# One program instead of two for the expert mixer of each layer of a decoder trunk

## The reference

```python
q = (xc @ w_q).reshape(ch, PEER_HEADS, 2, half)              # 8 heads, two halves of 128
s = jnp.einsum('thpd,hpnd->thpn', q, sub_keys)               # 128 keys a half
v1, i1 = lax.top_k(s[:, :, 0], PEER_TOPK)                    # 16 best of each half
v2, i2 = lax.top_k(s[:, :, 1], PEER_TOPK)
cand = (v1[..., :, None] + v2[..., None, :]).reshape(ch, PEER_HEADS, PEER_TOPK * PEER_TOPK)
vals, ci = lax.top_k(cand, PEER_TOPK)                        # 16 experts of 16384 for each token and head
e = (jnp.take_along_axis(i1, ci // PEER_TOPK, axis=-1) * N_KEYS + jnp.take_along_axis(i2, ci % PEER_TOPK, axis=-1))
g = jax.nn.softmax(vals, axis=-1)
act = jax.nn.gelu(jnp.einsum('td,thkd->thk', xc, u_tab[e])) * g
return jnp.einsum('thk,thkd->td', act, v_tab[e])
```

## Time and profile before

| | us |
|---|---|
| median of 3 runs (lowest, highest) | 3793.93 (3787.05, 3796.61) |
| the profiled execution | 3791.96 |
| its span, first to last instruction | 3790.2 |
| TensorE busy | 3232.8 (85%) |
| VectorE busy | 2058.1 (54%) |
| GpSimd busy | 1852.5 (49%) |
| ScalarE busy | 1267.4 (33%) |
| 768 scatters of gates, line 1700 | 1237.8, of one 1.612 |

### The profile page before, as it was taken

The page is one execution under the profiler, slowest core; times in us unless marked ns, Lnnn a source line. Parts: engine busy times, 40 slices in busy tenths (PEclk is TensorE's granted clock), DMA queues, the critical chain, the costliest instruction groups (busy, mean ns, idle before and its releaser), DMA issues. The chain is left out here.

```text
span 3790.2 us, 47486 instructions
## 1 busy us (share of the span) xinstructions
PE 3232.8 (85%) x14962; PEld 2615.9 (69%) x14962; DVE 2058.1 (54%) x4064; ACT 1267.4 (33%) x1877; POOL 1852.5 (49%) x1315
## 2 busy tenths in 40 slices
PE   8769999601999999999799889999503999999999
PEld 6558888501888888888566568888403888888887
DVE  4546677500322488888436637767400222588888
ACT  3433434200343333333325623443200222333333
POOL 0002887877870355555000004887877750455553
PEclk9889999855999999999899989999756999999999
DMA  9313656423674699999831014665423664799998
GB/s 334 123 68 115 133 123 139 86 0 30 144 182 153 228 349 351 354 351 333 293 109 45 12 38 123 147 130 124 70 0 55 144 187 146 265 349 354 349 352 295
DMA packets 396864, 680.85 MB, mean 180 GB/s; under 512 B 145008, under 2 KB 237168, under 8 KB 396528
## 3 DMA queue, kind: packets, MB, share of 16 engines
q1 hardware_dynamic: 191728, 494.73, 38.5%
q0 software_dynamic: 155648, 134.82, 18.0%
q10 hardware_dynamic: 49408, 50.33, 4.0%
HBM read 559.79 MB, written 119.93 MB: 179 GB/s over the span
## 5 line engine op out<-in xcount | busy, mean ns | idle before, releaser
L1700 POOL DMA_INDIRECT gate_matrix<-pe_misc x768 | 1237.8, 1612 | 1147.0 <-DVE pe_misc L1999 851.6
L398 PE MATMUL up_ps<-up_hhi,up_hi 128*128 128x512 f32 x2048 | 800.3, 391 | 400.2 <-PEq L1741 400.2
L389 DVE TENSOR_TENSOR up_lo<-up_raw,up_hi 128x1024 fp32r<-128x1024 f32 x256 | 313.8, 1226 | 1129.9 <-ACT up_hi L385 1047.5
L398 PE MATMUL up_ps<-up_hlo,up_hi 128*128 128x512 f32 x2048 | 798.6, 390 | 0.0
L398 PE MATMUL up_ps<-up_hhi,up_lo 128*128 128x512 f32 x2048 | 798.2, 390 | 0.0
L398 PEld LDWEIGHTS up_ps<-up_hhi,up_hi 128*128 128x128 f32 x2048 | 385.5, 188 | 480.3 <-issue 401.0
L2173 PE MATMUL ex_psy<-ex_vh,ex_ah 128*128 128x512 f32 x1536 | 600.3, 391 | 6.3 <-DVE ex_al L2274 6.1
L2173 PE MATMUL ex_psy<-ex_vl,ex_ah 128*128 128x512 f32 x1536 | 597.9, 389 | 0.0
L2173 PE MATMUL ex_psy<-ex_vh,ex_al 128*128 128x512 f32 x1536 | 597.8, 389 | 0.0
L1718 POOL DMA_INDIRECT ex_gz<-gelu,ga_at x256 | 343.5, 1342 | 387.5 <-DMA gelu<-up_z 310.0
L406 ACT ACTIVATE up_z<-up_ps 128x512 f32<-128x512 f32 x256 | 153.3, 599 | 1122.7 <-PE up_ps L398 1089.8
(11 more groups left out here) (345 smaller groups left out, 3502.6 us busy)
## 6 DMA issues: line engine op xcount, KB each, us to landing
up_raw<-in_uT SPq DMA_DIRECT2D x256, 512.0 KB
ro_wq<-in_v SPq DMA_DIRECT2D x256, 512.0 KB
gelu<-up_z SPq DMA_DIRECT2D x256, 256.0 KB
gate_matrix<-ga_at ACTq DMA_DIRECT2D x16, 3072.0 KB, 19.1
pe_misc<-gelu SPq DMA_DIRECT2D x256, 192.0 KB
ex_gm<-gate_matrix SPq DMA_DIRECT2D x128, 384.0 KB
ro_wq<-in_peer_wq SPq DMA_DIRECT2D x32, 512.0 KB
gate_matrix<-pe_misc POOLq DMA_INDIRECT x768
```

The source lines that it names most:

```text
L389: dve.tensor_tensor(self.lo[:, a, :, :], self.raw[:, a, :, :], self.hi[:, a, :, :].bitcast(F32), ALU.subtract).then_inc(self.lo_ready.sem, 1)
L398: last = pe.matmul(self.ps[:, a, :], w[:, a, dc, :], h[:, dc, :], start=(dc == 0 and m == 0), stop=(dc == DC - 1 and m == 2))
L1700: pool.indirect_dma_start(gmat.rearrange("p k (t a) -> (p k t) a", a=1), bass.IndirectOffsetOnAxis(ap=to[:, j:j + 1], axis=0), gates[:, j: ...
```

## The change

`route` and `experts` become one function, `peer`, with one block. The body of `route` stands in front of that of `experts` on each engine, in the same order. The large buffers of `route` become views of buffers of `experts` (`gv`, `vh`, `vl` and the PSUM of the v products), the small ones are allocated as before. The first head has 4 u tiles (`R0`), so its queries of the next head come after two tiles, and 68 u tiles follow the heads. In the first head VectorE makes the four `up.low`s after its first, second, fifth and last step. ScalarE's exponentials come after the third tile there. GpSimd writes all heads in one loop, waits for the gates of each, and the 48 DMAs of head 0 carry no `compute_op`.

```diff
+R0 = 4
-G0 = PH * RT
+G0 = R0 + (PH - 1) * RT
-ROUTED = 6
+def tile(h, first=False):
+    return 0 if first else h * RT + (R0 - RT)
     def scatter(self, pool, gmat, to, gates, h):
-        if h > 0:
-            pool.wait_ge(self.scattered.sem, self.scattered.base + 16 * HW * h)
+        place = gmat.rearrange("p k (t a) -> (p k t) a", a=1)
+        if h == 0:
+            for j in range(HW):
+                pool.indirect_dma_start(place, bass.IndirectOffsetOnAxis(ap=to[:, j:j + 1], axis=0), gates[:, j:j + 1], None
+                                        ).then_inc(self.scattered.sem, 16)
+            return
+        pool.wait_ge(self.scattered.sem, self.scattered.base + 16 * HW * h)
         for j in range(h * HW, (h + 1) * HW):
...
-def experts(k, l, x, up, ga, misc, wq, zmat, gmat, to, gates, rope):
+def peer(k, l, x, up, ga, misc, wq, wq_loaded, zmat, gmat, to, gates, rope):
...
+        wqh, wql = (x[:, 0, :, :].rearrange("p a (c m) -> p a c m", c=DC) for x in (vh, vl))
+        flat = gv[:].rearrange("p b d -> p (b d)")
+        sc, sc2 = (flat[:, n * D:(n + 1) * D].rearrange("p (b t n) -> p b t n", b=2, t=TT) for n in range(2))
+        cand = flat[:, 2 * D:3 * D].rearrange("p (t a b) -> p t a b", t=TT, a=TOPK)
+        cand2 = flat[:, 3 * D:4 * D].rearrange("p (t a) -> p t a", t=TT)
+        hot = flat[:, 4 * D:5 * D].rearrange("p (n a) -> p n a", a=TOPK)
+        q = flat[:, 5 * D:6 * D].rearrange("p (b t) -> p b t", b=2)
+        sk = flat[:, 6 * D:6 * D + 2 * NK].rearrange("p (b n) -> p b n", b=2)
+        psq = psy[:, 0:2, :]
+        pss = psy[:, 2:4, :].rearrange("p b (t n) -> p b t n", t=TT)
...
         def _(pe):
+            def head(h, more, first=False):
+                n = R0 if first else RT
+                scores(h)
+                for j in range(n):
+                    up.product(pe, tile(h, first) + j, j % GT)
+                    if more and j == n // 2 - 1:
+                        queries(h + 1)
+            queries(0)
+            head(0, True, first=True)
+            with pe.Fori(1, PH - 1) as h:
+                head(h, True)
+            head(PH - 1, False)
...
         def _(pool):
-            for h in range(ROUTED, PH):
+            for h in range(PH):
+                pool.wait_ge(given.sem, given.done(h))
                 ga.scatter(pool, gmat, to, gates, h)
...
         def _(dve):
+                def low(j, of_first=None):
+                    if not first:
+                        up.low(dve, tile(h) + (GT + j), j % GT)
+                    elif of_first is not None:
+                        up.low(dve, tile(h, first) + (GT + of_first), of_first % GT)
+                drop_first_eight(pairs[:2])
+                low(0, 0)
+                drop_first_eight(pairs[2:])
+                low(1, 1)
+                next_eight()
+                low(2)
+                candidates()
+                low(3)
+                drop_best_eight()
+                low(4, 2)
+                next_best_eight()
+                shift(h)
+                low(5)
+                picks()
+                keys_of(0)
+                low(6)
+                keys_of(1)
+                give(h)
+                low(7, 3)
...
-            route(k, l, up, self.wq, self.wq_loaded, zmat, gmat, ga, to, gates)
-            experts(k, l, x, up, ga, self.misc, self.wq, zmat, gmat, to, gates, rope)
+            peer(k, l, x, up, ga, self.misc, self.wq, self.wq_loaded, zmat, gmat, to, gates, rope)
```

More of the change, by code:

```diff
@@ L2111, in _, with load_subkeys, load_queries @@
         def _(sp):
+            def load_subkeys(h, b):
+                sp.wait_ge(scored.sem, h * 2 + scored.free(b))
+                sp.dma_start(sk[:, b, :], subkeys[bass.ds(h * 2 + b, 1), :, :].rearrange("a p n -> p (a n)")
+                             ).then_inc(sk_loaded[b].sem, 16)
+            def load_queries(h, b):
+                sp.wait_ge(wq_lo.sem, (h - 1) * 2 + wq_lo.done(b))
+                sp.dma_start(wq[:, b, :, :], w[bass.ds(h * 2 + b, 1), :, :, :].rearrange("a p c m -> p (a c) m")
+                             ).then_inc(wq_loaded[b].sem, 16)
+            def head(h, more, first=False):
+                if more:
+                    for b in range(2):
+                        load_queries(h + 1, b)
+                for j in range(R0 if first else RT):
+                    up.load(sp, tile(h, first) + (GT + j), j % GT)
+                    if not (first and j == 0):
+                        up.keep(sp, zmat, tile(h, first) + (j - 1), (j - 1) % GT)
+                    if more and j == 1:
+                        for b in range(2):
+                            load_subkeys(h + 1, b)
+            for b in range(2):
+                load_subkeys(0, b)
+            head(0, True, first=True)
+            with sp.Fori(1, PH - 1) as h:
+                head(h, True)
+            head(PH - 1, False)
             def load_v(tile, a):
@@ new lines, in give @@
+            def give(h):
+                here = bass.ds(h * TOPK, TOPK)
+                place()
+                dve.scalar_tensor_tensor(out=spot[:, 0:TD, :], in0=at[:, 0:TD, :], scalar=float(SD),
+                                         in1=bc(token[:, 0:TD].unsqueeze(2), [P, TD, TOPK]), op0=ALU.mult, op1=ALU.add)
+                dve.tensor_scalar(spot[:, TD, :], at[:, TD, :], float(S), token[:, TD:TT], ALU.mult, ALU.add)
+                dve.drain()
+                dve.tensor_copy(to[:, bass.ds(h * HW, HW)], spot[:, 0:TD, :].rearrange("p t k -> p (t k)"))
+                dve.tensor_copy(ga.at_z[:, here], spot[:, TD, :])
+                dve.tensor_copy(ga.at_v[:, here], row[:])
+                dve.wait_ge(expd.sem, h + expd.done(0))
+                dve.tensor_reduce(total[:], share[:], AX.X, ALU.add)
+                dve.drain()
+                dve.reciprocal(total[:], total[:])
+                dve.drain()
+                dve.tensor_scalar(ga.gate[:, here], share[:, TD, :], total[:, TD:TT], None, ALU.mult)
+                dve.tensor_tensor(gates[:, bass.ds(h * HW, HW)].rearrange("p (t k) -> p t k", t=TD), share[:, 0:TD, :],
+                                  bc(total[:, 0:TD].unsqueeze(2), [P, TD, TOPK]), ALU.mult).then_inc(given.sem, 1)
+                dve.drain()
@@ L2241, in weigh @@
+            tokens()
+            for b in range(2):
+                low_queries(0, b)
+            for a in range(GT):
+                up.low(dve, a, a)
+            head(0, True, first=True)
+            with dve.Fori(1, PH - 1) as h:
+                head(h, True)
+            head(PH - 1, False)
             def weigh(i, half):
```

456 lines of the change are left out of this document (176 added, 280 removed).

## The result

| | before | after |
|---|---|---|
| median (lowest, highest) | 3793.23 (3787.05, 3796.61), 4 runs | 3531.64 (3528.59, 3532.38), 4 runs |
| span of the profiled execution | 3790.2 | 3530.2 |

The ratio is 0.9311, with a 95% interval of 0.9294 to 0.9327: faster by 261.6 us. The prediction was 3401 with a range of 3383 to 3465, so the direction held and the time is 131 us above the forecast and 67 above the range.

A forecast was written before the change was run, and what follows sets the result against it. TensorE and GpSimd were taken to work in turns, meeting at `route`'s end; without that the longer road sets the end. 3792.0 - 193.6 (layer 0) - 197.1 (layer 1) = 3401.3, kept as 3401, range 3383 to 3465.

The forecast's parts named there:

- TensorE's road: TensorE's u tiles and eight heads' queries and scores up to the first v product: end at 1082.9 and 3055.7.
- start of GpSimd, layer 0: GpSimd's first scatter of head 0 comes 13.8 us earlier, at 337.1, because VectorE gives the gates sooner.
- head 0 and the wait after it: GpSimd's 48 plain scatters at 1.03 each plus gaps, and the wait for their landing: 67.2 us a layer.
- heads 1 to 7: GpSimd's scatters with add in these heads: 3 x 98.4 + 4 x 94.7 in layer 0, 295.2 + 373.6 in layer 1.
- last scatter to first v product: Last landing, SP's issue, first gate tiles' landing, and product to split, after GpSimd's last scatter: 8.0 us.
- The barrier: TensorE's wait of 400.2 us in two pieces for the end of `route`'s program; joining the programs removes it.
- first head with 4 tiles: Four u tiles move behind the heads: GpSimd starts 13.8 us earlier, TensorE idles 5.4 us more a layer.
- rival B: VectorE bounds the heads: the 5.4 us stall returns in each of 8 heads, time 3473; chance 0.07.
- the new wait for each head's gates: GpSimd's wait before each head's scatters costs nothing: gates come every 56.5 us and are used up every 95.
- the adds: GpSimd's scatters with add: 98.4 us a head for heads 1 to 3, 94.7 for heads 4 to 7.
- Rival A: Plain scatters of head 0 cost GpSimd as much as adds, 31.2 us more a layer, time 3462; chance 0.14.
- the start of the v stage: Last stores wait in SP's queue behind the scatters: up to 2 us a layer; stage length otherwise untouched.

The follow-up runs named there:

- best version: The changed kernel with waits for landings before every sixteenth plain scatter of head 0 and two changed orders at the v products' start; 3457.96 us, ratio 0.9111.

## Why the prediction was wrong

The 130.7 us between the span forecast (3399.5) and the one measured, by the prediction's own steps. Layer 1 is put on the new time axis (less the 193.6 forecast to be saved in layer 0). The 9.4 is the 8.0 after the last scatter and the 1.4 by which TensorE's road was forecast later there.

| step | forecast | measured | us too low |
|---|---|---|---|
| start of GpSimd, layer 0 | 337.1 | 339.2 | 2.1 |
| head 0 and the wait after it | 67.2, 67.2 | 98.2, 103.7 | 31.0, 36.5 |
| heads 1 to 7 | 674.0, 668.8 | 702.2, 695.9 | 28.2, 27.1 |
| last scatter to first v product | 8.0, 9.4 | 7.5, 7.6 | -0.5, -1.8 |
| from there to the start of layer 1's scatters | 1030.4 | 1029.7 | -0.7 |
| v stage of layer 1 and the end | 537.4 | 546.2 | 8.8 |

*The barrier* was right: the wait for the program's end is gone, and no other of its size stands in its place. That alone brought 265 us. TensorE's road was nearly right too: without the slow stretch its last u product starts at 1087.5 (best version), against 1082.9 forecast; the change has 1129.2. The *first head with 4 tiles* came as worked out, scatters from 339.2 and one stall of 5.57 us, and rival B's further stalls did not come.

**The step that failed** is, in the prediction's words, "the new wait for each head's gates costs nothing, because gates come every 56.5 us", with "Only at head 1 is that near (gates at about 393, wanted at 404)". The term costed at zero measured 33.5 and 41.0 us of waiting. It rested on TensorE going on at full speed beside the scatters, and I had taken that from rows in which all scatters were adds: "Before and after the hole TensorE is at 100% and 1.00 with the scatters running beside it". For the plain scatter I asked what it costs GpSimd, bounded that from both sides and got it right (1.03 forecast, 1.028 measured). I did not bound what it does to the others. No row of before could have told it; but an operation that no row shows has an unknown effect on its neighbours too, and the range had no term for that. With adds there is no slow stretch (3508.7), with plain scatters alone in the old kernel there is (1.0032), and with pauses it goes (3468.83): three runs that leave little room for another cause than unbroken plain scatters. By what way they hold TensorE up is not shown.

**A term mis-sized:** the adds. I took 98.4 a head for heads 1 to 3 and 94.7 for 4 to 7; it was 100.3 and 99.4 over all seven. That is so without the slow stretch too: 692.3 for heads 1 to 7 in layer 0 of the best version. Rival A, the forecast for adds in head 0, is therefore 3462 where that kernel took 3508.7. (The 98.4 for such a head 0 is the rate of whole heads read from rows; the terms of the sum for the plain head give 96.2 at 1.635. Measured were 97.9 and 98.3.) Counted from the records of that kernel, in heads 1 to 7 of layer 0: the 135 adds with no VectorE instruction beside them took 1.541 and 0.002 more; the other 201 together 43 us more, half of it beside the splits of u tiles (line 394). In before the same sum is 23 us, with 169 beside nothing. Two of before's seven heads ran in the hole with VectorE idle, and the two that I read 94.7 from were written when selection was over. In the change the heads' selections and the scatters overlap otherwise, and more adds meet VectorE. Why an add beside a split costs 0.22 more here and 0.13 in before stays open. The Trainium skill, "DMA: Bandwidth & Descriptors", section SWDGE vs HWDGE vs iDMA, says that VectorE in a two-port mode locks GpSimd out of the memory of its descriptors. The trace agrees only in that nothing is added without VectorE: no run shows in which mode its instructions ran, and the 66 adds that lie mostly beside its drains are as much longer (15.9 us in all, 0.24 each).

**A term left out:** the start of the v stage. I allowed "up to 2 us a layer"; the stages took 532.7 and 535.0 against 528.2 and 528.5 before, mostly because of one hole of 5.6 and 5.8 us. I had seen that the last stores stand behind the wait for the scatters, and reckoned without the loads behind the stores. The new order takes the hole out: 10.9 us with waits every 16, 12.9 with waits every 8.

Had only the slow stretch been foreseen, the forecast would have been 3401 + 31.0 + 36.5 = 3469, just above the range. Of the best version's distance to the forecast, 57 us, 43 are the adds (18.3 and 24.7), and 13 are head 0 with its two waits.

## What to carry to other kernels

An edit that swaps the kind of an operation can pay where it is made and cost more elsewhere: try it alone in the old kernel (here 1.0032, slower), and read all engines in the time in which it runs. A view of that window by engine shows within one line that an engine with no wait of its own does a fifth of its work. Where long rows of small indirect writes are issued beside TensorE's work, break them up with a wait for landings, which took 1.4 to 4.5 us here. After every 8 and every 16 no profile has a slow stretch, and 16 is the faster of the two but near the shortest onset seen; at 24 it was luck. And price an operation by rows whose neighbours are those that it will have.

## What the runs showed of the hardware

- Plain indirect scatters of 128 single elements, one each 1.26 us (0.96 and 0.30), for 19 to 31 us and more on end, bring TensorE down to one instruction each 0.7 us or a multiple (matmuls 2.8 us apart; 0.23 otherwise), until 4 to 11 us after the last one. The granted clock still reads 1.00 in the first 4 to 6 us; over a whole stretch, in most of which TensorE stands idle, it reads 0.5 to 0.7. VectorE's, ScalarE's and GpSimd's own instructions keep their durations.
- What holds TensorE up was not found. What is seen is that its signals come late, by 8 and 24 us at the start of the slow stretch, while ScalarE's end a wait at once (its rounding ends at 364.05, VectorE's split starts at 364.08). The records speak against the transfers: a scatter's packets start mostly within 0.8 us of the instruction's end, and the DMA share is 0.12. They speak against the fetching of TensorE's program too: the few such transfers there (16 KB, one in 27 us while a loop is first run through) take 1 to 1.7 us, and the later slow stretch of the run that held head 0 back, from 421 on, has none beside it. A pause inside the slow stretch did not end it where TensorE had been slow for 12 us and more (waits at 391 and 373); in the second runs of the two kernels with a wait before scatter 24 matmuls followed each other at full pace for 4 to 11 us after it. One ahead of it put it off, by 24 us after 8 scatters. Long rows at a slower pace without pauses were not tried.
- An add costs GpSimd 0.58 us more than a plain scatter (1.541 and 0.96), and it is cut up otherwise. DMA packets of GpSimd's queue for the 48 scatters of head 0, first plain (changed kernel), then adds (head 0 with adds), as packets, MB, share of 16 engines:

```profile
q0 software_dynamic: 1536, 0.03, 1.7%
```
```profile
q0 software_dynamic: 6912, 0.03, 20.5%
```

- That is 32 packets a plain scatter and 144 an add, for the same 128 elements. The prediction had worked out from the Trainium skill, "DMA: Bandwidth & Descriptors", section SWDGE vs HWDGE vs iDMA, that by one pair of descriptors for each DMA operation a plain scatter would save nothing; the measurement says otherwise, with 1.028 against 1.612 for an add.
- The Trainium skill, "Perfetto Trace Analysis", section DMA Instruction — SWDGE (GPSIMD), says that a row of such a DMA ends when the descriptors are made and not when the data has moved; the trace agrees, with the packets of a plain scatter 0.6 to 0.8 us after the row's end.
